# A two-layer encoder trunk: modulation in one first stage for one shift and scale, the other chunks streamed during attention

## What is computed

```
mod = jnp.dot(jax.nn.silu(c), w_ada) + b_ada          # w_ada: 1024 x 6144 for each layer, 24 MB
sh1, sc1, gt1, sh2, sc2, gt2 = split(mod, 6)
hn = rmsnorm(x, g_mix) * (1 + sc1) + sh1
x = x + gt1 * token_mixers(hn, w_in, ..., w_out)      # 16 heads of three kinds, one output projection
hn = rmsnorm(x, g_ffn) * (1 + sc2) + sh2
x = x + gt2 * expert_choice_ffn(hn, w_router, w_gate, w_up, w_down)   # 16 experts, 64 tokens of each sequence
```

## Time and profile before

| | us |
|---|---|
| median of 3 runs | 2851.78 |
| lowest and highest run | 2846.72, 2856.35 |
| profiled execution, its own time | 2845.89 |
| its span | 2844.1 |
| PE busy in the span | 2489.2 |
| DVE busy | 1851.6 |
| ACT busy | 1294.7 |

### The profile page before, as it was taken

How to read it: one execution, slowest core, us unless ns; L and a number is a source line. 1 busy time by engine, 2 the same in 40 slices (tenths; PEclk the granted TensorE clock), 3 DMA queues, 4 the chain that set the end, 5 groups by cost and what they waited for, 6 DMA issues and landing times.

```text
span 2844.1 us, 31122 instructions
## 1 busy us (share of the span) xinstructions
PE 2489.2 (88%) x11606; PEld 1859.4 (65%) x11606; DVE 1851.6 (65%) x2946; ACT 1294.7 (46%) x2075; POOL 374.7 (13%) x253
## 2 busy tenths in 40 slices
PE   3798987989849999999758899798997699999993
PEld 1466775667738888888525577655676588888882
DVE  0346555465469999999505455454654999999994
ACT  0224323143227777777403243131431577777771
POOL 1002000110011111211000110001100011111112
PEclk7797988988769999999868988898977799999997
DMA  9803014020169999999694111132001899999994
GB/s 318 284 1 111 23 45 137 1 82 28 40 252 367 390 388 390 387 388 374 218 373 139 66 46 45 67 93 82 16 30 72 331 378 388 389 391 386 387 376 153
DMA packets 204900, 599.37 MB, mean 211 GB/s; under 512 B 36094, under 2 KB 50702, under 8 KB 204720
## 3 DMA queue, kind: packets, MB, share of 16 engines
q1 hardware_dynamic: 183936, 522.21, 48.9%
q0 software_dynamic: 15824, 58.27, 7.3%
q10 hardware_dynamic: 4992, 16.92, 1.6%
HBM read 555.62 MB, written 43.84 MB: 211 GB/s over the span
## 4 chain that ended last, share of the span: by engine, by line
PE 76%; DVE 10%; DMA 7%; issue 3%; ACT 2%; POOL 1%; POOLq 0%; SPq 0%; ACTq 0%; PEld 0%; DVEq 0%; PEldq 0%
PE bank L1318 12%; PE bank L1320 12%; PE bank L1319 12%; PE bank L1179 7%; DMA ring_w<-in_w_ada 6%; PE bank L1227 5%; PE bank L1208 5%; PE bank L1217 3%; PE bank L1251 3%; PE bank L1253 2%; PE bank L1252 2%; PE bank L1175 2%; PE bank L1177 2%; PE bank L1176 2%; PE bank L1271 1%
## 5 line engine op out<-in xcount | busy, mean ns | idle before, releaser
L997 DVE TENSOR_TENSOR feed_lo<-feed,feed_hi 128x1024 fp32r<-128x1024 f32 x768 | 887.9, 1218 | 83.5 <-ACT feed_hi L649 81.8
L649 ACT ACTIVATE feed_hi<-feed 128x1024 fp32r<-128x1024 f32 x768 | 749.3, 1050 | 202.8 <-PE bank L1320 100.3
L1227 PE MATMUL bank<-V,pbuf 128*128 128x64 f32 x1664 | 253.7, 297 | 27.7 <-ACT pbuf L619 16.9
L1227 PEld LDWEIGHTS bank<-V,pbuf 128*128 128x128 f32 x1664 | 240.7, 219 | 45.1 <-ACT pbuf L619 29.8
L1179 PE MATMUL bank<-ring,hT 128*128 128x512 f32 x512 | 230.1, 604 | 0.0
L611 ACT ACTIVATE pbuf<-pbuf,smin 128x256 f32<-128x256 f32 (+2 forms) x192 | 117.3, 611 | 238.4 <-DVE smin L845 238.4
L410 POOL TENSOR_TENSOR stat<-stat,neg_half 128x1 f32<-128x1 f32 (+2 forms) x88 | 70.5, 802 | 1087.0 <-DVE stat L913 485.6
L1318 PE MATMUL bank<-feed_hi,hid_hi 128*128 128x512 f32 x512 | 205.0, 400 | 9.1 <-DVE hid_lo L1019 9.1
L1318 PE MATMUL bank<-feed_hi,merged_hi 128*128 128x512 f32 x512 | 206.8, 404 | 1.1 <-DVE merged_lo L1004 1.1
L1318 PE MATMUL bank<-feed_hi,xe_hi 128*128 128x512 f32 x512 | 205.2, 401 | 0.0
L1320 PE MATMUL bank<-feed_hi,merged_lo 128*128 128x512 f32 x512 | 202.9, 396 | 0.0
(11 more groups left out here) (183 smaller groups left out, 4120.5 us busy)
## 6 DMA issues: line engine op xcount, KB each, us to landing
feed<-in_w_gate SPq DMA_DIRECT2D x64, 2048.0 KB, 11.3
feed<-in_w_up SPq DMA_DIRECT2D x64, 2048.0 KB, 10.7
feed<-in_w_down SPq DMA_DIRECT2D x64, 2048.0 KB, 10.5
ring_w<-in_w_ada SPq DMA_DIRECT2D x24, 2048.0 KB, 16.5
ring<-in_w_in SPq DMA_DIRECT2D x16, 2048.0 KB, 13.4
ring<-in_w_out SPq DMA_DIRECT2D x8, 2048.0 KB, 10.5
X<-residual ACTq DMA_DIRECT2D x24, 512.0 KB, 3.5
residual<-X POOLq DMA_DIRECT2D x16, 512.0 KB, 2.9
```

Of the source, the lines that this page charges most:

```text
L649: act.activation(feed_hi[q % HIGHS][:, kk, :], feed[q % FEED][:, kk, :], ACT.Copy).then_inc(feed_hi_ready, 1)
L997: dve.tensor_tensor(feed_lo[q % FEED][:, kk, :], feed[q % FEED][:, kk, :], full(feed_hi[q % HIGHS][:, kk, :]), ALU.subtract).then_inc(feed ...
L1227: ins = pe.matmul(bank[5 + oc // 512][:, oc % 512:oc % 512 + HD], pbuf[:, 3 + m % 2, b * P:(b + 1) * P], V[:, lo + b, vc:vc + HD], start=( ...
```

## The change

The first stage keeps four of the twelve loads of layer 0, those of `sh1` and `sc1`. The other eight chunks of 512 columns of layer 0 are loaded and multiplied during the attention of sequence 0, two slots for each: `ada_sum` (eight products) in slot 2n + 2 and `ada_turn` (four small ones) in slot 2n + 3, both through `bank[7]`. Layer 1 has no first stage: its chunks 0 to 3 are handled in the same way during sequence 1 of layer 0, its chunks 4 to 11 during its own sequence 0. A chunk comes as two halves of 1 MB into the two halves of `ring0`, which is free once the projection is done. Each half is requested when its predecessor has been used. The transposition and the store of the four row vectors (`mod_turn`) move to slot 19 of sequence 0, and the loads of `gate` and `rows2` wait for them. In sequence 0 SP issues chunk 0, then `w_out`, then the other chunks, then the rows; in sequence 1 `w_out`, the rows, then the chunks. The skewed table of layer 1 is written during sequence 1 of layer 0, into a pad of its own; the other small loads of layer 1 are issued behind the first four gathers of layer 0's experts. The copy of the second sequence's input moves behind the mask of the bias in the first attention stage. The first loads wait for nothing. The first stage's products wait for the bias and gain vectors of both layers.

```diff
+FIRST_ADA = 4
+ADA_SLOT = (4, 5, 2, 3)
...
+def streamed(layer, s):
+
+    if s == 0:
+        return list(range(FIRST_ADA, 12))
+    return list(range(FIRST_ADA)) if layer + 1 < LAYERS else []
...
-def schedule():
+def schedule(layer, s):
 
     out = []
     for k in range(SLOTS):
         out.append(("slot", k // 16, k))
+        for n, c in enumerate(streamed(layer, s)):
+            out += [(name, c, k) for at, name in ((2 * n + 2, "ada_sum"), (2 * n + 3, "ada_turn")) if at == k]
+        if s == 0 and k == 19:
+            out.append(("mod_turn", 0, k))
         for i in range(TILES):
             out += [(name, i, k) for at, name in AFTER if 16 * i + at == k]
+    return out
...
@@ SyncE @@
+            def load_first(n):
+
                 cols, rows = 1024 * (n // 2), 4 * (n % 2)
-                sp.dma_start(ring_w[j][:, :, :],
-                             ada_v[bass.ds(layer, 1), :, rows:rows + 4, cols:cols + 1024].rearrange("o p k f -> (o p) k f"))\
-                    .then_inc(slot_loaded[j], 16)
+                sp.dma_start(ring_w[ADA_SLOT[n]][:, :, :], ada_v[0, :, rows:rows + 4, cols:cols + 1024])\
+                    .then_inc(slot_loaded[ADA_SLOT[n]], 16)
+
+            def load_out(layer):
+
+                for n in range(2):
+                    load(4 + n, out_v, layer, n)
+
+            def load_ada(layer, s):
+
+                for n, c in enumerate(streamed(layer, s)):
+                    t = ada_turns(layer, s) + n
+                    if s == 0 and n == 1:
+                        load_out(layer)
+                    for h in range(2):
+                        if n:
+                            sp.wait_ge(ada_used, 2 * (t - 1) + h + 1)
+                        sp.dma_start(ring_a[h][:, :, :], ada_v[layer + s, :, 4 * h:4 * h + 4, 512 * c:512 * c + 512])\
+                            .then_inc(ada_in[h], 16)
...
+            for n in range(FIRST_ADA):
+                load_first(n)
...
+                        if it == 0 and n >= 2:
+                            sp.wait_ge(first_used, n + 1)
+                        elif s == 0 and layer:
+                            all_fed(layer - 1, n)
+                        elif n == 0 and it:
+                            sp.wait_ge(ada_used, 2 * ada_turns(layer, s))
+                        elif n == 1 and it:
+                            sp.wait_ge(row_used, it)
+                        elif it:
+                            sp.wait_ge(out_used, it)
+                        load(n, in_v, layer, n)
...
+                    sp.wait_ge(proj_used, it + 1)
+                    if s == 0:
+                        load_ada(layer, s)
...
@@ GpSimd @@
-            pool.wait_ge(slot_loaded[3], 16)
-            pool.dma_start(x_d[SEQ:SEQS * SEQ, :], x[SEQ:SEQS * SEQ, :]).then_inc(scattered, 16)
...
+            def skew(layer):
+
+                pad = pads[layer]
+                pool.memset(pad[:, :], 0.0).then_inc(pad_ready, 1)
+                pool.wait_ge(pad_ready, layer + 1)
+                pool.dma_start(pad[:, 48:48 + COL_OFF],
+                               rpb[layer:layer + 1, :, :, :].rearrange("l h r c -> (l h r) c")).then_inc(skew_in, 16)
+                pool.wait_ge(skew_in, layer * 16 + 16)
+                pool.dma_start(skew_d[:, :, :], pad[:, :].unsqueeze(1).to_broadcast([4 * ROW_OFF, GRID, 128])).then_inc(skew_out, 16)
...
+                if s and layer + 1 < LAYERS:
+                    pool.wait_ge(proj_used, it + 1)
+                    skew(layer + 1)
+                if it == 0:
+                    pool.dma_start(x_d[SEQ:SEQS * SEQ, :], x[SEQ:SEQS * SEQ, :]).then_inc(scattered, 16)
...
+            skew(0)
+            prepare(0)
+            meet(epoch(0, 0))
...
+                if layer + 1 < LAYERS:
+                    prepare(layer + 1)
...
@@ ScalarE @@
+            for layer in range(LAYERS):
+                rows = hT[1][:, layer, :]
+                for src, at, n in ((b_ada, R_BIAS, 48), (g_mix, R_GMIX, 8), (g_ffn, R_GFFN, 8), (g_grp, R_GGRP, 8)):
+                    act.dma_start(rows[at:at + n, :], src[layer:layer + 1, :].rearrange("o (k p) -> (o k) p", p=P))\
+                        .then_inc(rows_in, 16)
...
+                    if kind == "mod_turn":
+                        act.wait_ge(side_full, side_at[kind, i])
+                        act.activation(mod_st[:, :], bank[7][0:64, 0:P], ACT.Copy).then_inc(side_free, 1)
+                        act.wait_ge(side_free, side_at[kind, i])
+                        act.dma_start(mod_d.rearrange("m s p -> (m s) p"), mod_st[:, :]).then_inc(mod_out, 16)
...
@@ VectorE @@
+                    if kind == "ada_sum":
+                        dve.wait_ge(side_full, side_at[kind, i])
+                        dve.tensor_copy(abuf[:, :], bank[7][:, :]).then_inc(side_free, 1)
+                    if kind == "ada_turn":
+                        at = layer + s
+                        dve.wait_ge(side_full, side_at[kind, i])
+                        chain.add(dve.tensor_copy(mods[:, 4 * i:4 * i + 4, :], bank[7][:, 0:4 * SEQS].rearrange("p (m s) -> p m s", s=SEQS)))
+                        dve.sem_inc(side_free, 1)
+                        ins = dve.tensor_tensor(mods[:, 4 * i:4 * i + 4, :], mods[:, 4 * i:4 * i + 4, :],
+                                                bc(rows_t[:, at, R_BIAS + 4 * i:R_BIAS + 4 * i + 4], SEQS), ALU.add)
+                        for sc, g in ((M_SC1, R_GMIX), (M_SC2, R_GFFN)):
+                            if 4 * i + 4 == sc + 8:
+                                chain.add(ins)
+                                ins = with_gain(at, sc, g)
+                        ins.then_inc(mods_ready, 1)
...
@@ TensorE @@
+            def first_ada():
+                pe.wait_ge(rows_in, LAYERS * 64)
+                for layer in range(LAYERS):
+                    ins = pe.transpose(bank[0][:, R_END * layer:R_END * layer + R_END], hT[1][0:R_END, layer, :], ident[0:R_END, 0:R_END])
+                ins.then_inc(vec_turned, 1)
...
+                    pe.wait_ge(slot_loaded[ADA_SLOT[n]], 16)
...
+                    if kind == "ada_sum":
+                        n = ada_at + streamed(layer, s).index(i)
+                        side_turn(i)
+                        for h in range(2):
+                            pe.wait_ge(ada_in[h], 16 * n + 16)
+                            for j in range(4):
+                                ins = pe.matmul(bank[7][STRIP * j:STRIP * j + STRIP, :], silu_c[:, SEQS * (4 * h + j):SEQS * (4 * h + j) + STRIP],
+                                                ring_a[h][:, j, :], start=(h == 0), stop=(h == 1))
+                            ins.then_inc(ada_used if h == 0 else side_full, 1)
+                        side += 1
+                    if kind == "ada_turn":
+                        side_turn(i)
+                        pe.sem_inc(ada_used, 1)
+                        for m in range(4):
+                            ins = pe.matmul(bank[7][:, SEQS * m:SEQS * m + SEQS], abuf[:, m * P:(m + 1) * P], summed, start=True, stop=True)
+                        ins.then_inc(side_full, 1)
+                        side += 1
+                    if kind == "mod_turn":
+                        side_turn(i)
+                        pe.wait_ge(mods_ready, 8)
+                        pe.transpose(bank[7][0:64, 0:P], mods[:, M_GT1:M_END, :].rearrange("p m s -> p (m s)"), ident).then_inc(side_full, 1)
```

More of the change, by code:

```diff
@@ L102, with ada_turns, epoch @@
 SLOTS = 16 * (TILES - 1) + AFTER[-1][0] + 1
+def streamed(layer, s):
+    if s == 0:
+        return list(range(FIRST_ADA, 12))
+    return list(range(FIRST_ADA)) if layer + 1 < LAYERS else []
+def ada_turns(layer, s):
+    return sum(len(streamed(a, b)) for a in range(LAYERS) for b in range(SEQS) if (a, b) < (layer, s))
+def epoch(layer, stage):
+    return 1 + layer * (SEQS + 2) + stage
 def chunks(i):
@@ L120, in schedule, with sides @@
         out.append(("slot", k // 16, k))
+        for n, c in enumerate(streamed(layer, s)):
+            out += [(name, c, k) for at, name in ((2 * n + 2, "ada_sum"), (2 * n + 3, "ada_turn")) if at == k]
+        if s == 0 and k == 19:
+            out.append(("mod_turn", 0, k))
         for i in range(TILES):
             out += [(name, i, k) for at, name in AFTER if 16 * i + at == k]
+    return out
+SIDE_END = ("ada_sum", "ada_turn", "mod_turn", "merged_0", "merged_1", "out_03", "out_13", "normed_0", "normed_1", "router_1")
+def sides(layer, s):
+    out = {}
+    for kind, i, k in schedule(layer, s):
+        if kind in SIDE_END:
+            out[kind, i] = len(out) + 1
     return out
@@ L344, in _ @@
                 for s in range(SEQS):
-                    turn = layer * TURNS + s + 2
+                    it = layer * SEQS + s
                     for n in range(MIX_CHUNKS):
-                        load(n, turn, in_v, layer, n)
+                        if it == 0 and n >= 2:
[9 more added lines that the diff above has]
+                        load(n, in_v, layer, n)
@@ L356, in _ @@
```

(24 more changed lines are left out.)

208 lines of the change are left out of this document (84 added, 124 removed).

## The result

The changed kernel takes 2826.68 us in the median of 20 runs (2812.46 to 2856.07), the kernel before 2848.43 beside it (2830.97 to 2860.64): ratio 0.9933, 95% interval 0.9912 to 0.9955. That is faster by more than 0.3%, and 3 us from the forecast of 2830. The profiled execution took 2833.76 (span 2832.0), 12.1 less than the 2845.89 of before.

A forecast was written before the change was run, and what follows sets the result against it. It took DMA transfers to bound the modulation stages and PE the attention stages. 2845.9 − 124.5 saved + 80 for steps + 24.3 first waits + 1 gave 2826.7, put at 2830 us; range 2806 to 2866.

The forecast's parts named there:

- First stage: Layer 0's start: with four loads kept, the fourth lands at 46 and the first norm comes at 57, saving 50 us.
- Layer 1: From layer 0's last expert product to layer 1's norm: some 19 us instead of 94.6, saving 75.5 us.
- The steps: Streamed chunks' products and turns on PE in attention slots: 4.2 us each, 80 us (61 to 103) for nineteen.
- first waits: PE waiting for chunks: 3.8 us in layer 0's first stage, 18.7 plus a 1.8 turn in its second; 24.3 in all.
- the loop: Slots 2 to 17 at full clock: turn, half-chunk load and its products set a 7.6 us period, adding 3.2 a step.
- The clock in the slots: Slots 2 to 18 of a first attention stage: granted clock between 0.6 and 0.9, a mixture of half and full.
- the slower rival: Slots with steps all at half clock: 5.4 us a step instead of 4.2, total 2866; chance 0.20.
- Late weights: Projections: w_in loads land 10 us late in both layers, 20 us go back, total 2850; chance 0.08.
- 124.5: Total saved in us: 50 in layer 0's first stage and 75.5 at layer 1's norm, after the small loads' charge.
- The 1 us for the small loads: Layer 1's small loads behind the first four gathers of layer 0's experts on POOL's queue: charged 1 us (0 to 5).

The follow-up runs named there:

- the second run with copies: Kernel before the change, with 20, 15, 10 and 5 one-column ScalarE copies ahead of the last turned keys of the four stages; 2838.31 us, run once.
- the early release: Changed kernel, with the second half chunk's place given back once its products have read it, not at the turn one slot later; ratio to before 0.9899.
- The second pair and the order of loads: Changed kernel, with a second pair of half buffers for the streamed chunks and SyncE's loads reordered to suit; ratio to before 0.9788, median 2792.38 us.
- the run with the chunk first: Changed kernel, with SyncE issuing the first chunk ahead of w_out and the rows in layer 0's second stage; ratio to before 0.9888, median 2815.42 us.
- the run whose norm was at 38.3: Changed kernel, other transfers held until layer 0's fourth w_ada load landed, table and small loads on SyncE behind w_in loads; ratio to before 0.9890, median 2820.04 us.
- the two further executions of before's work: Kernel before the change, with 5, 10, 15, 20 or 20, 15, 10, 5 one-column ScalarE copies in the four stages; 2849.07 and 2838.31 us, once each.

## Why the prediction was right, point by point

**First stage.** Landing 46 forecast, 45.67 measured; norm 57 forecast, 54.8 measured. The 9.2 from the last load to the norm, not the 11, was the right value (9.1), though the last burst took the 3.64 of half clock. The reason, that other transfers take the difference to 30.2, is shown: with them held back the load is used at 27.5 to 27.9.

**Layer 1.** 18.7 us from the last product to the norm, 19 forecast.

**The steps: right in sum, wrong in kind.** 80 and 24.3 were forecast, 104.3 in all, and 99.3 came; slots 2 to 18 of the first stage took 70.4, within the 65 to 75 that were named. That the sum fits is partly luck. The 4.2 us a step, between 3.2 at full and 5.4 at half clock, put nearly all of it down to PE's work, with 0.3 us a step for waiting at full clock. Measured: 1.6 a step for the work, 22.8 for the first waits, and 44 for the loads in the loop, 2.2 a step, of which about half is idle time and half the lower clock that comes with it. Two terms were mis-sized, in opposite directions. The work was priced as an addition to slots at 0.50, which the earlier trace rows shows for part of them only (0.64 in all); with the steps and without the loads they ran at 0.93 and 0.97. Slots without steps take 30.4 at 1.00 in the second run with copies, and (51.3 − 30.4) / 8 = 2.6, near the 2.9 of the earlier trace rows. And the loop was drawn through the turn, which the early release shows to be of little weight; what costs is that a single pair can be loaded again only after use. The second pair and the order of loads take 40.6 of the 66.9 us that are not PE's work, in the two first stages 22.0 of 42.0; what the rest needs beyond the rate of the transfers (0.90 busy) was not tried.

**The clock in the slots.** "Between 0.6 and 0.9": 0.84, 0.77, 0.83. The Trainium skill's rule ("TensorE: Matmul & The Clock Gate", "Loop structure matters more than you think") has the clock fall where matmuls stand behind a long wait for a DMA. The trace agrees in the direction: 0.84 and 0.83 with the waits, 0.93 and 0.97 without. It does not agree with the price that the forecast drew from it: half clock throughout, the slower rival, did not come.

**First waits.** 3.8 forecast for the second chunk, 6.2 measured, nothing in layer 1, 2.2 measured (start 1588.41). In the second stage of layer 0 PE was to be idle for about 15 us, and was for 16.6. (The forecast's terms have the chunk whole at 600.3, 590.4 + 4.8 + 5.1, and not at 602.) That the chunk's place behind `w_out` and the rows causes it is shown: SyncE issued `w_out` at 562.0 and came to the chunk only at 582.3. That the table does is not: in the run with the chunk first the first wait was gone, and 9.5 us were left for the second chunk, behind `w_out`.

**Late weights.** The projections took 127.5 to 128.2, not more than before (127.8 to 128.8): that rival was wrong here. It came true in the run whose norm was at 38.3 (133.1).

**What was left out.** Nothing was forecast for the stages after slot 18, and they took 17 us more in the profiled pair. The steps need not be the cause: without them the rests were 185.8 and 191.5, and in the two further executions of before's work 185.5 to 191.0; the 179.9 and 179.7 are the lowest of all the profiles taken. Some 7 to 10 of the 17 us belong to the two executions that were profiled, which are 12.1 apart where the medians are 19 (by the ratio) to 22 apart. The rest stays in the medians too, as it does without the steps (118 us where the stretches give 126.7), and its cause is not shown. Without the 17 us the forecast would have had 124.5 against 126.4 and 104.3 against 99.3, so it promised some 7 us too little gain; that the median came within 3 us of it is partly luck. The 1 us for the small loads stands twice in the forecast's sum, in the 124.5 and behind it.

## What to carry to other kernels

Work moved under a stage cost less here through its engine time (32 us) than through the places its operands are loaded into (67): count how many loads are in flight while one is used, and give a streamed operand a second set before trimming its release. Order each queue by who is wanted first, and look at what a barrier drains before holding loads back. Price added PE work at the clock that the stretch will have with it, not at today's.

## What the runs showed of the hardware

The granted clock of a stretch is not a property of its instructions. Slots 36 to 44, 139 to 142 products, took 22.5 us at 1.00 or 26.3 to 28.1 at 0.76 to 0.82, and in the same stage of the kernel before 26.5 in one execution and 22.5 in another; slots 0 to 18 without steps 30.4 to 37.9. PE stands idle ahead of the last turns before slot 0 in stages of either kind (7.10 us in the 0.76 of before, 7.17 in the 1.00 of the second run with copies), so that pause alone does not tell them apart; what decides at which point the clock falls is open. Nor does a busy PE keep it up: before, from 238.0 to 253.9, PE was busy 15.71 of 15.90 us at 0.50. The executions of one kernel spread with the clock: those of the changed kernel reach from 2812 us at a mean clock of 0.908 to 2846 at 0.892.

Small loads that spread one row over 128 partitions (32 KB each) landed 15.1 to 25.3 us after their issue where `w_ada` went ahead alone, and GpSimd's drain at the barrier waited for them.
